# A hybrid decoder layer on one core: the last chunk's routing ahead of other work, the embedding product spread over three experts, weight homes filled at other times, small vectors laid out in rows

## The reference

```
proj = x @ w_in                                  # 1024 -> 2568 columns
x1 = LN1(2**0.25 * x + [pool_group | mlstm_group] @ w_out)
logits = x1 @ w_router + b_router                # top 4 of 32 experts, softmax over the four
ff = sum over the chosen experts: gate * (swiglu(x1 @ w1[e] + b1[e]) @ w2[e] + b2[e])
x2 = LN2(2**0.25 * x1 + ff)
y  = x2 + sigmoid(x2 @ w_ple_gate) * (p @ w_ple) # p: a 256-wide embedding per token
```

## Time and profile before

| | |
|---|---|
| median of 3 runs | 1109.31 us (1108.20 to 1110.46) |
| the profiled execution | 1109.61 us, its span 1107.8 us |
| PE busy | 1075.3 us, 97% of the span |
| DVE, ACT, POOL busy | 39%, 14%, 7% |
| read from DRAM | 436.6 MB, 398 GB/s over the span |
| granted TensorE clock | 1.0 throughout |

### The profile page before, as it was taken

How to read it: one execution, slowest core, us unless ns; L and a number is a source line. 1 busy time by engine, 2 the same in 40 slices (tenths; PEclk the granted TensorE clock), 3 DMA queues, 4 the chain that set the end, 5 groups by cost and what they waited for, 6 DMA issues and landing times.

```text
span 1107.8 us, 15186 instructions
## 1 busy us (share of the span) xinstructions
PE 1075.3 (97%) x5608; PEld 428.8 (39%) x5608; DVE 437.3 (39%) x1109; ACT 159.4 (14%) x306; POOL 78.9 (7%) x107
## 2 busy tenths in 40 slices
PE   9999999999999999999999999999999999999998
PEld 7786433333333333333333333333333333333334
DVE  1648663333333333333333333333333333332245
ACT  1532341000000000000000000000000000000033
POOL 0747420000000000000000000000000000000000
PEclk9999999999999999999999999999999999999999
DMA  9979999999999999999999999999999999999961
GB/s 317 269 308 399 294 361 393 430 426 427 428 431 428 427 429 429 428 427 431 428 427 428 429 429 427 430 429 428 427 429 428 427 426 429 427 426 429 426 259 40
DMA packets 52624, 440.63 MB, mean 398 GB/s; under 512 B 10560, under 2 KB 17980, under 8 KB 27397
## 3 DMA queue, kind: packets, MB, share of 16 engines
q1 hardware_dynamic: 51545, 439.00, 95.8%
q0 software_dynamic: 368, 0.57, 0.2%
q10 hardware_dynamic: 676, 0.59, 0.2%
HBM read 436.61 MB, written 3.77 MB: 398 GB/s over the span
## 4 chain that ended last, share of the span: by engine, by line
PE 58%; DMA 23%; DVE 9%; SPq 5%; issue 2%; POOL 1%; ACT 1%; DVEq 0%; POOLq 0%
PE bank L999 25%; DMA ring<-in_w_mlp 22%; PE bank L1070 16%; PE bank L958 4%; DVE proj L1629 3%; PE bank L1150 3%; PE bank L778 3%; DVE proj L1626 2%; DVE proj L1624 2%; PE bank L1051 1%; SPq L378 1%; PE bank L971 1%; POOL ring L2107 1%; PE bank L993 1%; PE bank L1059 1%
## 5 line engine op out<-in xcount | busy, mean ns | idle before, releaser
L999 PE MATMUL bank<-ring,proj 128*64 128x512 f32 x2024 | 460.9, 597 | 14.1 <-DMA ring<-in_w_mlp 13.4
L1590 DVE SCALAR_TENSOR_TENSOR xT<-bank,proj,xT 128x512 f32<-128x512 f32 x128 | 90.2, 747 | 423.7 <-PE bank L958 422.4
L999 PEld LDWEIGHTS bank<-ring,proj 128*64 128x64 f32 x2024 | 140.6, 136 | 290.0 <-issue 261.9
L1070 PE MATMUL bank<-ring,pool_side 128*64 128x512 f32 x1024 | 226.8, 595 | 0.4 <-ACT pool_side L1963 0.4
L1070 PEld LDWEIGHTS bank<-ring,pool_side 128*64 128x64 f32 x1024 | 71.3, 137 | 133.5 <-issue 129.1
L1957 ACT ACTIVATE proj<-proj 128x256 f32<-128x256 f32 x64 | 26.7, 417 | 546.1 <-DVE proj L1623 545.1
L1581 DVE TENSOR_SCALAR proj<-bank,ln_rows_of_pairs 128x64 f32<-128x64 f32 x256 | 67.5, 337 | 24.5 <-PE bank L971 24.5
L958 PE MATMUL bank<-mixT 64*128 64x512 f32 x264 | 74.5, 641 | 0.9 <-ACT mixT L1966 0.5
L599 PE MATMUL bank<-xT,ring 128*128 128x264 f32 x320 | 74.3, 388 | 0.2 <-ACT proj L1776 0.2
L599 PEld LDWEIGHTS bank<-xT,ring 128*128 128x128 f32 x320 | 60.0, 190 | 12.3 <-issue 1.6
L937 PE MATMUL bank<-xreg,proj 128*64 128x512 f32 x248 | 58.7, 592 | 0.0
(11 more groups left out here) (369 smaller groups left out, 632.6 us busy)
## 6 DMA issues: line engine op xcount, KB each, us to landing
ring<-in_w_mlp SPq DMA_DIRECT2D x190, 2048.0 KB, 29.4
ring<-in_w_in SPq DMA_DIRECT2D x9, 1024.0 KB, 14.4
ring<-in_w_out SPq DMA_DIRECT2D x4, 1024.0 KB, 9.5
ring<-in_w_ple_gate SPq DMA_DIRECT2D x4, 1024.0 KB, 29.3
xreg<-in_x_prompt SPq DMA_DIRECT2D x4, 512.0 KB, 4.7
ring<-q_row SPq DMA_DIRECT2D x1, 2048.0 KB, 7.3
ring<-k_row SPq DMA_DIRECT2D x1, 2048.0 KB, 7.0
out<-ring SPq DMA_DIRECT2D x1, 2048.0 KB, 15.7
```

The lines of the kernel that those rows point to most:

```text
L999: last = pe.matmul(bank[q][BLOCK * t:BLOCK * (t + 1), :], xgT[:, k % 4, k // 4, :], rows_[:, col:col + 512], start=False, stop=(k == KD - 1))
L1070: last = pe.matmul(bank[4][BLOCK * h:BLOCK * (h + 1), :], aT[:, m, BLOCK * t:BLOCK * (t + 1)], w[:, k % 2, 512 * h:512 * h + 512], start=F ...
L1590: ins = STT(total[:, c, s], ins_bank[h][:, :], gate_table[:, c, bass.ds(n, 1)], total[:, c, s], ALU.mult, ALU.add)
```

## The change

1. **Chunk 1's routing.** The counts of the early chunks (`EARLY_PLACES`) now stand ahead of `turn_quarter(0)` and `turn_quarter(1)` on PE, and the other counts ahead of `router(1, 6)`; before, all of them stood behind it.
2. **Embedding.** The four half steps of `early_embedding` and `early_samples` move from the routing stage into experts 0, 1 and 2, which are written out ahead of the loop for it, on PE and on ACT. Their banks change to 2 and 3, and `early_pT` gets space of its own beside `gates`. PE waits for ACT's copy before each gather of experts 0 to 2.
3. **Homes.** `load_late(0)` stands behind the first two w_out loads, `load_late(2)` behind the second load of x, and `load_late(1)` behind pair 46 in the stream of weights, after `ple_ps` 3.
4. **Small vectors.** `ln1_cols` (two loads of 1024 single elements) goes; the router weights are loaded in the order of pairs, in runs of 256 bytes and not 128; `ln2_cols` is loaded early by SP in runs of four elements and not by POOL in single ones during expert 0. w_ple_gate is loaded in runs of 8 KB a partition and not of 4 KB. To fit, PE transposes every second column of x1 and every fourth of x2.
5. **Others.** These loads stand behind w_out and `late[0]`, ahead of the q row. POOL's copy of 14 state rows from DRAM to DRAM moves to the start of its later work. DVE's copy of the samples' v (`sbc_done`) moves ahead of `head(0)`.

```diff
@@ SP
-            sp.dma_start(wrout[:, :, :], w_router[0].rearrange("(k p) e -> p k e", p=P)).then_inc(sem("wrout_in"), 16)
-            sp.dma_start(brout[:, :], b_router).then_inc(sem("wrout_in"), 16)
-            for i, src in enumerate((ln1_g, ln1_b)):
-                sp.dma_start(ln1_cols[:, i, :], src[0].rearrange("(k p) -> p k", p=P)).then_inc(sem("wrout_in"), 16)
...
             load_w_out(0)
             load_w_out(1)
+            load_late(0)
+            sp.dma_start(wrout[:, :, :].rearrange("p (m a) e -> p m (a e)", a=2),
+                         w_router[0].rearrange("(m p a) e -> p m (a e)", p=P, a=2)).then_inc(sem("wrout_in"), 16)
+            sp.dma_start(brout[:, :], b_router).then_inc(sem("wrout_in"), 16)
...
+            for i, src in enumerate((ln2_g, ln2_b)):
+                sp.dma_start(ln2_cols[:, i, :].rearrange("p (h a) -> p h a", a=4),
+                             src[0].rearrange("(h p a) -> p h a", p=P, a=4)).then_inc(sem("ln2_cols_in"), 16)
...
+            sp.wait_ge(sem("pool_ps"), 4)
+            sp.wait_ge(sem("z_ready"), 4)
+            load_late(2)
             sp.wait_ge(sem("rest_cleared"), 1)
...
-            load_late(0)
-            load_late(2)
...
-            sp.wait_ge(sem("ple_ps"), 3)
-            load_late(1)
             for n in range(SLOTS, UNITS * STEP, 2):
                 sp.wait_ge(sem("units_used"), n - SLOTS + 2)
                 load_next(n)
+                if n == SLOTS + 30:
+                    sp.wait_ge(sem("ple_ps"), 3)
+                    load_late(1)
@@ PE
+            def pair_columns(rows_, kk):
+
+                return rows_.rearrange("p (m x a) -> p m a x", m=4, a=2)[:, kk // 2, kk % 2, :]
...
             mix(1, second, range(6, KD), (1,))
-            turn_quarter(0)
-            turn_quarter(1)
-            router(1, 6)
...
                       start=False, stop=True).then_inc(sem("pos_ps"), 1)
+            turn_quarter(0)
+            turn_quarter(1)
             pe.matmul(bank[3][:, 0:3 * EXPERTS], ones16[0:1, :], far_row, start=True, stop=False)
             count_places(0, (1,))
             count_places(2, (1,))
+            router(1, 6)
             logit_rows(2)
-            pe.wait_ge(sem("ple_in"), 16)
-            early_samples()
...
             count_places(1, ()).then_inc(sem("pos_ps"), 1)
-            early_embedding(0, (0,))
...
+                    if opening and j < 2 and k in (1, 3):
+                        early_embedding(j, (k // 2,))
                     if k == 1:
...
                         combine(2, (j + 1) % 2)
-
+                        if opening and j == 2:
+                            pe.wait_ge(sem("hotT_done"), 3)
+                            early_samples()
+
+                if opening and j < 3:
+                    pe.wait_ge(sem("ple_done"), j + 1)
...
-            early_embedding(0, (1,))
-            early_embedding(1, (0, 1))
             pe.wait_ge(sem("places_split"), 1)
-            pe.wait_ge(sem("ple_done"), 1)
...
-            with pe.Fori(0, npass * EXPERTS - 2 * STEP, STEP) as n:
+            pe.wait_ge(sem("ple_in"), 16)
+            for j in range(STEP):
+                expert(j, j, opening=True)
+            with pe.Fori(STEP, npass * EXPERTS - 2 * STEP, STEP) as n:
...
                     for k in range(4):
-                        kk = 4 * half + k
                         last = pe.transpose((bank[7], bank[4])[half][:, k * P:k * P + n],
-                                            final(c, n)[:, kk * P:(kk + 1) * P], ident[0:n, 0:n])
+                                            final(c, n).rearrange("p (h x a) -> p h a x", h=2, a=4)[:, half, k, :],
+                                            ident[0:n, 0:n])
@@ DVE
-            head(0, hout[:, 0], den)
             dve.wait_ge(sem("sbc_ps"), 2)
             step(dve.tensor_copy(scol[:, 1, :], bank[6][:, STATES:2 * STATES]), "sbc_done")
+            head(0, hout[:, 0], den)
@@ POOL
-            pool.wait_ge(sem("total_ready"), 2)
-            for i, src in enumerate((ln2_g, ln2_b)):
-                pool.dma_start(ln2_cols[:, i, :], src[0].rearrange("(k p) -> p k", p=P)).then_inc(sem("ln2_cols_in"), 16)
```

More of the change, by code:

```diff
@@ L179, in build @@
                    for c in range(2)]
-        gates = sb("gates", [2 * HEADS, TOK])
+        gate_space = sb("gate_space", [P, 2 * (P + SAMPLES)])
+        gates = gate_space[0:2 * HEADS, 0:TOK]
+        early_pT = gate_space[:, :].rearrange("p (k n) -> p k n", k=2)
         gcol = small[:, 0:28]
@@ L214, in build @@
         ln2_cols = small[:, 126:142].rearrange("p (s k) -> p s k", s=2)
-        ln1_cols = small[:, 142:158].rearrange("p (s k) -> p s k", s=2)
         ln1_shift = [stat[:, 58 + c:59 + c] for c in range(3)]
@@ L263, in build @@
         places = part(3 * 2 * EXPERTS).rearrange("p (c r e) -> p c r e", c=3, r=2)
-        early_pT = part(2 * (P + SAMPLES)).rearrange("p (k n) -> p k n", k=2)
         assert off[0] <= TILES * TOK
@@ L537, in _ @@
                 sp.dma_start(ring[:, 6 + i, :].rearrange("p (k n) -> p k n", k=2),
-                             w_ple_gate[0, 256 * i:256 * i + 256, :].rearrange("(k p) n -> p k n", p=P))\
+                             w_ple_gate[0, 512 * (i // 2):512 * (i // 2) + 512, :]
+                             .rearrange("(p a) n -> p a n", a=4)[:, 2 * (i % 2):2 * (i % 2) + 2, :])\
                   .then_inc(sem(f"pgate_in{i}"), 16)
@@ L768, in turn_quarter @@
                     kk = 4 + 2 * quarter + k
-                    last = pe.transpose(QUARTERS[quarter][:, k * P:k * P + P], xtok[:, 1, kk * P:(kk + 1) * P], ident)
+                    last = pe.transpose(QUARTERS[quarter][:, k * P:k * P + P], pair_columns(xtok[:, 1, :], kk), ident)
                 last.then_inc(sem("x1T_ps"), 1)
@@ L982, in landed, with expert @@
                     pe.wait_ge(sem(f"slot{s}"), i4 * 12 + 16 * (before[s] + landings(u) - missing))
-            def expert(n, j, closing=0):
+            def expert(n, j, closing=0, opening=False):
                 i4 = n - j
@@ L1670, in _ @@
             begin_sum(total[:, 0, :], 0, "total_ready")
-            dve.wait_ge(sem("ple_ps"), 3)
             dve.wait_ge(sem("dve_chain"), counts["dve_chain"])
@@ L1942, in _ @@
             ln1_rows(2, 1, 6)
-            act.wait_ge(sem("ple_ps"), 1)
-            act.copy(embedded_samples, EMBED_BANKS[2][0][:, 0:256]).then_inc(sem("ple_done"), 1)
             def embedded_early(half):
-                act.wait_ge(sem("ple_ps"), half + 2)
+                act.wait_ge(sem("ple_ps"), half + 1)
                 act.copy(embedded_rows[:, 512 * half:512 * half + 512], EMBED_BANKS[1][half][:, :]).then_inc(sem("ple_done"), 1)
@@ L1970, in _ @@
             warm = stat[:, 57:58]
-            embedded_early(0)
+            act.nop().then_inc(sem("out_done"), 1)
             for i in range(3):
@@ L1996, in _ @@
             npass = act.value_load(extra[0:1, 0:1], min_val=0, max_val=PASSES - 1) + 1
-            with act.Fori(0, npass * EXPERTS - STEP, STEP) as n:
+            for j in range(STEP):
+                if j < 2:
+                    embedded_early(j)
+                elif j == 2:
+                    act.wait_ge(sem("ple_ps"), 3)
+                    act.copy(embedded_samples, EMBED_BANKS[2][0][:, 0:256]).then_inc(sem("ple_done"), 1)
+                expert(j, j)
+            with act.Fori(STEP, npass * EXPERTS - STEP, STEP) as n:
                 for j in range(STEP):
@@ L2109, in by_states @@
                 pool.wait_ge(sem("pool_chain"), chain[0])
+            pool.dma_start(pool_sample[0, :, 0:HIST - 1, :], state_pool[0, :, 1:HIST, :]).then_inc(sem("small_out"), 16)
             pool.wait_ge(sem("cq_in"), 32)
```

30 lines of the change are left out of this document (12 added, 18 removed).

## The result

The changed kernel takes 1114.58 us, median of five executions (1113.74 to 1117.91), against 1108.79 for the kernel before in the same job (1108.2 to 1110.46). The ratio is 1.0052, 95% interval 1.0040 to 1.0064: slower by 5.8 us. I had said 1110.2 us, and 1114.0 at most. The execution that was profiled is the longest of the five: span 1116.1 us, time 1117.91. The mean granted clock of the five is 0.994 in it, 0.995 in those of 1115.73 and 1114.58 us, and 0.998 in the two shortest.

A forecast was written before the change was run, and what follows sets the result against it. The end was taken as the end of the weight stream plus PE's fixed rest of 59.7 us. Terms -3.0 + 2.45 + 0.8 + 0.3 + 0.3 = +0.85 gave a median of 1110.2 us, range 1105.5 to 1114.0.

The forecast's parts named there:

- the start of expert 0: End of the routing stage: less embedding and earlier counts let expert 0 start at 147.9 us and not 151.42, -3.5 us.
- The first stage: Work up to the routing: a later q row and transposes of every second column, +0.3 us.
- The route's gain: Chunk 1's routing: with the early counts ahead of the turns, `turned(0)` starts about 1.3 us earlier than 148.38.
- The cover: Expert 0: its own 1.9 us of embedding is covered by the earlier start, so w2 starts 1.3 us earlier.
- pair 36: Weight pair followed through the stream: predicted to land at 212.6 us and not 215.6, -3.0 us.
- Home 1: `late[1]` loaded behind pair 46 adds 1 MB to a full weight stream, +2.45 us.
- The tail: After the last expert's w2: 24 transposes of x2 at every fourth column, +0.3 us, at most +3.0.
- Instruction loads: Four experts written out bring some 5 more instruction loads into the stream, +0.8 us, between 0 and 3.0.
- A: Rival: the stream keeps the whole early start, pair 36 lands before 211 us, -3.2 us, 1106.3 us; chance 0.24.
- B: Rival: tail transposes of columns four apart cost 0.236 us each, +3.0 and not +0.3, 1112.9 us; chance 0.20.
- C: Rival: instruction fetches all hit the slowest engine, or the q row is 2.5 us late, 1112.4 us; chance 0.12.
- D: Rival: chunk 1's route is off expert 0's path, `turned(0)` stays at 148.38, 1111.5 us; forecast with it 0.44.

The follow-up runs named there:

- experiments 4: The changed kernel with the embedding back in the routing stage, home 1 ahead of the stream and no experts written out; 1110.62 us, ratio 1.0008 to the kernel before.
- experiment 6: The kernel before with only home 1's load moved from the hole ahead of the stream to behind pair 46; 1111.97 us, ratio 1.0022.
- experiment 8: The kernel before with only POOL's two single-element loads of ln2's vectors moved from 166 us to behind the router's weights; 1117.94 us, ratio 1.0076.
- experiment 3: The kernel before with only the embedding moved into experts 0 to 2, four experts written out and home 1 behind pair 46; 1116.18 us, ratio 1.0059.
- experiment 13: The changed kernel with 1.25 us of dummy matmuls in PE's waits; 1113.91 us over six executions, ratio 1.0040 to the kernel before.
- experiment 7: The kernel before with only the early counts ahead of chunk 1's last turns and its router behind those counts; 1108.84 us, ratio 0.9993.
- experiment 10: The kernel before with only the first four experts written out for PE and ACT ahead of their loops; 1109.96 us, ratio 1.0005.
- experiment 11: The kernel before with only homes 0 and 2 filled earlier, home 1 as before; 1113.56 us over four executions, ratio 1.0043.

## Why the prediction was wrong

**The bound was right.** The end is the end of the weight stream plus PE's fixed rest: in every profile w2 of the last expert follows the stream, and what a part costs ahead of pair 16 comes out at the end.

**The step that failed is the start of expert 0**, "expert 0 starts at about 147.9 and not 151.42: -3.5 us", and in it "`turned(0)` starts about 1.3 us earlier". It started at 152.75, and my own sign of being wrong, later than 149, came true. Four things are in it.

*The clock.* I added up what leaves PE and took it as time gained, at a clock that stays. What remains from 139 to 142.7 are transposes, the router and counts, none wider than 128 columns. PE is busy 2.50 of 3 us there and waits 0.39 us at the longest. Here the clock falls, and not in the changed kernel alone: experiments 4, 6 and 8, with the embedding in its old place, have such a fall too, for 3.4 us each. What the move changes is its length. Without the embedding it lasts 13.7 us, and in experiment 3 13.6, so that the gathers and the start of expert 0 are done at 1.2 GHz. The Trainium skill (TensorE: Matmul & The Clock Gate, HAM oscillation — how this bites in real kernels) puts such falls down to long gaps in which PE is idle, and its next section, A second HAM failure mode, to frequent short ones. The first agrees with experiment 8 at 98.2 us, in a wait of 4.83 us. Just ahead of the falls between 141 and 150 us no wait is over 0.59 us; whether short waits or narrow work bring those about, no run here separates. My prediction had no rival for this. In the profiled execution it is the difference between spans of 1116.1 and 1111.8, 4.3 us; between the medians of the changed kernel and of the three executions of experiment 13 at full clock (1112.6), 2.0 us.

*The first stage.* I had +0.3 us for it. The mix ends at 139.1 and not 138.05, by 0.4 us of a later L626 and 0.46 us of the samples' transposes, and at 139.4 in experiment 13: +1.0 and +1.4.

*The route's gain.* At full clock `turned(0)` starts at 148.67, 9.3 us behind the end of the mix, where it was 10.3: 1.0 us gained, with the samples' embedding gone from ahead of the gather, and I had 1.3. The first stage has used it up: `turned(0)` is 0.3 us later than before. Alone the route gives 0.3 us (experiment 7).

*The cover.* I had PE start expert 0 as soon as `turned(0)` allowed, and did not see a wait for issue of 0.63 to 0.80 us ahead of the biases, which the embedding had covered: experiment 10, with the same experts written out and the embedding in its old place, has no such wait. First w1 at full clock is 150.06, 1.4 us earlier than before and not 3.5. The 1.9 us of embedding inside expert 0 then outweigh it: w2 starts at 173.25, 0.5 us later. My step from first w1 to w2 was right (23.6 us predicted, 23.2 seen); it hung on the start. So pair 36 gains 0.3 us where I had 3.0, and pair 38, landed at 220.9 against 220.4, loses 0.4.

**The other terms.** *Home 1*: +2.45 predicted, +2.4 in the profile and in experiment 6. *Small vectors and the q row*: L626 at 86.99 lies in my 86.6 to 87.2, though this start differs by itself from profile to profile, 86.10 to 86.81 in kernels that are alike up to there. The price of +0.01 us for a transpose of every second column holds for 128 rows (0.63 us for four and not 0.60), not for the eight rows of the samples: 0.058 us each, 1.12 and not 0.66 us for eight. *The tail*: +0.6 and not +0.3, nearly all of it the same thing, the samples' eight transposes with 1.05 us and not 0.59. *Instruction loads*: +0.8 predicted, and experiment 10 has them at nothing. The Trainium skill (Runtime: NRT & Kernel Launch, Instruction fetch mechanics) has them "mostly hidden"; the runs agree, with 5 more loads and 832.7 us against 832.6. The +1.4 us between pair 36 and the end is mostly the gap to pair 38, as said above, and belongs to the start; the rest is within what this stretch differs by between profiles of other kernels (831.2 us in experiment 7, 832.6 before).

**The rivals.** A fell: pair 36 landed at 219.5, or 215.3 at full clock. B fell by its own mark, the group of eight at 0.95 us and not near 1.9. Weight loads of transposes in the changed kernel, ns as min/median/max, first and last start:

```profile
L1149 PEld LDWEIGHTS bank<-cst,xT x16: 195/210/213, 1077.0 to 1086.4; 128*128 128x128 f32 x16
L1149 PEld LDWEIGHTS bank<-cst,xreg x8: 190/213/213, 1091.0 to 1091.8; 8*128 8x128 f32 x8
```

Every fourth column loads in 210 ns, every second in 207; the rule on lines of 16 bytes (the Trainium skill, SBUF — State Buffer, Door 1: The DMA port swizzle) would have made the one slower than the other, and the trace doesn't show it. The jump is between columns side by side and either of these, 141 to some 210 ns. The eight rows pay nearly all of it (0.058 of 0.07 us each) and 128 rows little; probably their matmuls are too short to cover a load, which was not tested. C decides at L626 later than 88, and it is at 86.99, and its extra loads cost nothing (experiment 10); experiment 11 shows that it was a real danger, at 88.24 with home 0 ahead of the q row and the vectors as they were. D comes nearest: `turned(0)` is no earlier at full clock. With D's start I should have been at 1111.5, and the executions at full clock took 1111.7 to 1113.6.

**What stays open.** What brings the clock down, and why in some executions and not in others. At a mean clock of 1.0 executions of one kernel still differ by 2 us and more; a short fall may hide in the rounding, and a mean doesn't say where a fall lies. Experiments 3 and 11 are 1 to 2 us slower than their parts add up to.

## What to carry to other kernels

Dense work that stands in a stage of short, dependent operations does two things: it takes PE's time and, here, it brought the clock back after 3.4 us where it otherwise stayed down for 13.6. Before it is moved away, read the granted clock in the mean of several executions and not of the profiled one alone, and price what comes behind at half the clock. Half a us of filler in waits may be worth a trial: the kernel with it has a median 0.9 us lower and no long executions, in another job. Compare a start between two profiles only from a point that both reach alike. A load of single elements is priced at the engine that issues it, too, above all where a second follows: place it where nothing stands behind it in that queue. And work moved into a stream's first step is free only if that step really starts earlier by as much; add up the waits on issue that the old work covered.

## What the runs showed of the hardware

- The granted clock fell to 1.2 GHz behind a stretch with PE busy 83% (2.50 of 3 us) and no wait over 0.39 us, when its work was transposes, router and counts of at most 128 columns. In experiments 4, 6 and 8 it was back after 3.4 us, with the samples' embedding and a gather behind the fall; in the changed kernel and in experiment 3, with the gather alone, after 13.7 and 13.6 us. Whether it falls differs from one execution to the next of one program.
- A transposed tile read at every second or fourth column: 207 and 210 ns for the weight load, 141 for columns side by side. For 128 rows the pace goes from 0.110 to 0.119 us each, for 8 rows from 0.083 (0.66 / 8) to 0.140 (1.12 / 8).
- Two loads of 1024 single elements issued by POOL, one behind the other: the second is issued 6.86 us (experiment 8) and 7.56 us (kernel before) after the first instruction has ended. A product behind the second followed at once.
